# Expert down weights shared out among the DMA engines by neighbouring rows, in a two-layer streaming encoder

## The reference, cut to what matters

```python
def _swiglu(x, wa, wb, wc):
    return (jax.nn.silu(x @ wa) * (x @ wb)) @ wc
...
    for e in range(N_EXPERTS):
        y = y + comb[:, e:e + 1] * _swiglu(x, we1[e], we3[e], we2[e]).astype(f32)
```

## Time and profile before

| what | value |
|---|---|
| runs, us | 2668.35, 2989.45, 2655.33; median 2668.35 |
| the profiled execution, us | 2659.83 |
| its span, us | 2658.1 |
| TensorE busy | 2288.2 us (86%) |
| VectorE busy | 1534.9 us (58%) |
| ScalarE busy | 1157.2 us (44%) |
| memory read and written | 456.31 MB and 26.97 MB |
| chain that ended last, product lines L847 | 52% and 2% for L851 |

### The profile page before, as it was taken

The page is one execution under the profiler, slowest core; times in us unless marked ns, Lnnn a source line. Parts: engine busy times, 40 slices in busy tenths (PEclk is TensorE's granted clock), DMA queues, the critical chain, the costliest instruction groups (busy, mean ns, idle before and its releaser), DMA issues.

```text
span 2658.1 us, 37593 instructions
## 1 busy us (share of the span) xinstructions
PE 2288.2 (86%) x14153; PEld 1975.6 (74%) x14153; DVE 1534.9 (58%) x2150; ACT 1157.2 (44%) x1553; POOL 184.2 (7%) x257
## 2 busy tenths in 40 slices
PE   6899985778699989897999867587999999999991
PEld 3899753548599989897997635386878878878871
DVE  0456637323543444344566374336888888888884
ACT  3332113322443423333321134315777677777773
POOL 2000101101000000000000011100000100100104
PEclk7699766858799999996998678697999999999995
DMA  7122525351254444541223143305999999999993
GB/s 243 51 80 64 167 60 173 131 180 57 72 166 119 150 127 138 141 144 32 64 80 104 57 145 114 126 11 217 339 382 360 351 377 352 348 383 367 340 358 137
DMA packets 285625, 485.57 MB, mean 183 GB/s; under 512 B 21550, under 2 KB 216632, under 8 KB 285504
## 3 DMA queue, kind: packets, MB, share of 16 engines
q1 hardware_dynamic: 264816, 416.42, 45.3%
q0 software_dynamic: 20688, 67.44, 7.3%
HBM read 456.31 MB, written 26.97 MB: 182 GB/s over the span
## 4 chain that ended last, share of the span: by engine, by line
PE 54%; DVE 6%; DMA 6%; issue 3%; ACT 3%; POOL 1%; DVEq 0%; ACTq 0%; PEld 0%; PEldq 0%; POOLq 0%; SPq 0%
PE banks L847 52%; DMA expert_ring<-in_we 4%; PE banks L851 2%; ACT region_split L1572 1%; DVE region L2092 1%; DVE expert_lower L2092 1%; DVE weights_lower L2092 1%; DVE hidden_t L2092 1%; DVE scratch L2092 1%; ACT hidden_t L1572 0%; DVE region_split L2092 0%; DMA hidden_t<-h_rows,pass_tokens 0%; DMA scratch<-bias_rows 0%; DVE weight_ring L2092 0%; ACT scratch L1572 0%
## 5 line engine op out<-in xcount | busy, mean ns | idle before, releaser
L847 PE MATMUL banks<-upper_parts,region_split 128*128 128x320 f32 x1664 | 397.1, 314 | 37.0 <-DVE weights_lower L2092 29.3
L2092 DVE TENSOR_TENSOR expert_lower<-expert_ring,region_split 128x1408 fp32r<-128x1408 f32 (+1 forms) x270 | 388.6, 1467 | 28.1 <-ACT region_split L1572 18.5
L847 PE MATMUL banks<-upper_parts,weights_lower 128*128 128x320 f32 x1248 | 390.6, 313 | 0.0
L847 PE MATMUL banks<-region_split 128*128 128x320 f32 (+1 forms) x1376 | 376.6, 337 | 12.9 <-DVE upper_parts L2092 12.9
L1572 ACT ACTIVATE region_split<-expert_ring 128x1408 fp32r<-128x1408 f32 (+1 forms) x270 | 331.9, 1257 | 63.2 <-DMA expert_ring<-in_we 63.1
L847 PEld LDWEIGHTS banks<-upper_parts,region_split 128*128 128x128 f32 x1664 | 290.0, 192 | 38.8 <-DVE weights_lower L2092 35.8
L847 PE MATMUL banks<-region_split,upper_parts 128*128 128x512 f32 (+1 forms) x996 | 304.1, 382 | 1.4 <-DVE upper_parts L2092 1.4
L847 PE MATMUL banks<-z_weights_upper,upper_parts 128*128 128x256 f32 (+3 forms) x844 | 264.2, 342 | 22.6 <-DVE region_split L2092 22.5
L847 PE MATMUL banks<-expert_lower,upper_parts 128*128 128x512 f32 x720 | 271.4, 377 | 0.0
L847 PEld LDWEIGHTS banks<-region_split 128*128 128x128 f32 x1376 | 245.3, 189 | 28.8 <-issue 13.5
L1572 ACT ACTIVATE region_split<-weight_ring 128x2048 fp32r<-128x2048 f32 (+2 forms) x72 | 141.0, 1960 | 252.5 <-PE banks L847 225.2
(11 more groups left out here) (306 smaller groups left out, 3569.8 us busy)
## 6 DMA issues: line engine op xcount, KB each, us to landing
expert_ring<-in_we SPq DMA_DIRECT2D x240, 704.0 KB, 8.3
expert_ring<-in_we SPq DMA_DIRECT2D x165, 512.0 KB, 4.6
weight_ring<-in_w_ada SPq DMA_DIRECT2D x48, 1024.0 KB, 7.4
weight_ring<-in_w SPq DMA_DIRECT2D x88, 512.0 KB, 4.4
weight_ring<-in_w_in SPq DMA_DIRECT2D x24, 1024.0 KB, 5.3
weight_ring<-in_w SPq DMA_DIRECT2D x16, 1408.0 KB, 6.3
weight_ring<-in_w_out SPq DMA_DIRECT2D x8, 1024.0 KB, 8.8
y_rows<-hidden_t POOLq DMA_DIRECT2D x15, 512.0 KB, 7.5
```

What stands on the lines that cost most here:

```text
L847: return nc.tensor.matmul(out, lhsT, rhs, start=first, stop=last)
L2092: return v.tensor_tensor(out, x, y, op)
```

## The change

Two places. On SP, the down tiles' source is now a view with three dimensions: 16 groups (i), 8 rows in each (j), 1024 columns. Element (i, j) is row 128 f + 16 j + i of the expert's down weights, and it goes to partition 8 i + j. So a tile still has the same 128 rows of 4,096 B and goes to the same place of the ring, but its rows stand in another order: partitions 0 to 7 hold rows 0, 16, 32, ... 112 of the block, partitions 8 to 15 rows 1, 17, ... and so on.

On VectorE, the gated product's hidden columns are stored in that same order: position 8 i + j of block f holds hidden column 128 f + 16 j + i. Both inputs are read with a step of 16 elements for eight elements and then from the next column on; the output is contiguous. After the transpose partition 8 i + j of the turned product meets the row of the down tile that belongs to it.

The number of instructions and their order is the same on every engine. The 33 down loads in SP's program have one dimension more, and the three multiplications read with steps; nothing else differs.

```diff
--- before.py
+++ after.py
@@ -609,21 +609,23 @@
             l = DEPTH - 1
             sp.wait_ge(stage_done, 3 * (STAGES.index(f"out{l}") + 1))
             sp.wait_ge(slots_ready, 1)
-            by_row = [a[x][l // 2, :, :, :].rearrange("e (k p) n -> e p k n", p=P) for x in ("we1", "we3", "we2")]
+            by_row = [a[x][l // 2, :, :, :].rearrange("e (k p) n -> e p k n", p=P) for x in ("we1", "we3")]
+            down_rows = a["we2"][l // 2, :, :, :].rearrange("e (f j i) n -> e i j f n", j=8, i=16)
             n.add("expert_used", 1 - NPLACE)
             q = 0
 
             def expert_rows(e, up):
 
                 nonlocal q
-                w1, w3, w2 = (x[bass.ds(e, 1), :, :, :].rearrange("e p k n -> p (e k) n") for x in by_row)
-                for src in [w[:, k, :] for k in range(KD) for w in (w1, w3)] if up else [w2[:, f, :] for f in range(NF)]:
+                w1, w3 = (x[bass.ds(e, 1), :, :, :].rearrange("e p k n -> p (e k) n") for x in by_row)
+                w2 = down_rows[bass.ds(e, 1), :, :, :, :].rearrange("e i j f n -> i j (e f) n")
+                for src in [w[:, k, :] for k in range(KD) for w in (w1, w3)] if up else [w2[:, :, f, :] for f in range(NF)]:
                     if q >= NPLACE:
                         sp.wait_ge(expert_used, n.value("expert_used"))
                     n.add("expert_used")
                     place = q % NPLACE
                     q += 1
-                    sp.dma_start(ER[:, place, 0:src.shape[1]], src).then_inc(expert_in[place], 16)
+                    sp.dma_start(ER[:, place, 0:src.shape[-1]], src).then_inc(expert_in[place], 16)
 
             def expert_of(at):
                 return sp.value_load(PASSES[0:1, bass.ds(at, 1)], min_val=0, max_val=NE - 1)
@@ -2664,7 +2666,9 @@
                         for part, (first, end) in enumerate(PARTS):
                             take(silu_made)
                             take(ups_summed)
-                            tt(PRODUCT[:, first:end], SGM[:, first:end], PS[:, 3 + part, 0:end - first], ALU.mult)\
+                            turned = lambda x: x.rearrange("p (f j i) -> p f i j", j=8, i=16)
+                            tt(PRODUCT[:, first:end].rearrange("p (f i j) -> p f i j", j=8, i=16), turned(SGM[:, first:end]),
+                               turned(PS[:, 3 + part, 0:end - first]), ALU.mult)\
                                 .then_inc(product_made, 1)
 
                     def down(rows, products, following):
```

## The result

The changed kernel takes 2733.5 us at the median (2728.2 to 2741.2, four runs), the kernel before 2671.0 us beside it. The ratio, which leaves out one slow run of the kernel before (2989.5 us), is 1.0229, with an interval of [1.0185, 1.0272]: some 61 us slower. The forecast, 2638 us, has the wrong sign, and the time lies above its range, the high end of 2710 included. What happened has the signs of the rival of the landing side. The profiled execution took 2741.2 us, its span 2739.5 us.

What follows compares the result with a forecast made beforehand. TensorE was taken as the bound, stopped once a pass by late loads. From 2659.8 us, 21 for shorter stops and 3 for clock came off, 2 went back for strided reads: 2638 us, range 2618 to 2710 (forecast's own 2618 to 2655).

Steps and rivals of the forecast that it cites:

- What bounds the kernel before: Expert stage: TensorE bounds, 48.0 us of own work in a 50.64 us pass, stopping once a pass for late loads.
- the stops: TensorE's once-a-pass waits, 2.1 us each; shrinking them was to save 21 us, plus 3 us of low clock.
- (a): Down-tile loads: the new row order lifts them from 312 to 412 GB/s at full share, saving 21 us.
- landing-side rival: Down loads' writes: eight neighbouring partitions per engine make engines collide; under 300 GB/s decides, up to 2775 us; chance 0.33.
- In step half of the time: Landing-side rival's middle case: down tiles at 275 GB/s, 52.4 us of DMA a pass, 2685 to 2700 us.
- Engines drift apart: Argument against the landing-side rival: in a queue never empty, engines drift apart and then seldom meet.
- (b): Issue of down loads on SP: 40 ns more each, 0.4 us a pass, hidden by the queue's waits for TensorE.
- (c): VectorE's three strided gated products: +0.5 us a pass taken, +0.9 at most, hidden in 3.55 us of idle time.
- (d): Transposes, roundings and matrix products: same shapes and order, only the sum over rows reordered; no effect.
- VectorE becomes the bound: Rival: products grow 0.9 us a pass with nothing hiding them, 12 us in all, 2671 us; chance 0.05.
- Nothing: Rival: engines don't share loads as written, or down tiles' slowness comes from issue gaps; 2650 to 2668 us; chance 0.20.

Runs made afterwards that it cites:

- e1: The change's down loads with the gated product made as before (down part's result wrong), against the kernel before: ratio 1.0211.
- e10: All eleven down tiles in 16 groups of 8, ten with each group's rows adjacent in memory, product as before, against the kernel before: ratio 1.0237.
- e4: Down tiles' rows 11 apart from partition to partition, in the plain split of 128, TensorE turning every 11th product column, against the kernel before: ratio 0.9981.
- e7: Ten of eleven down tiles read 5,632 B from each row address, 4,096 B apart, against the kernel before: ratio 0.9953.
- e8: ScalarE and VectorE split the product's last part before the fourth up tile instead of behind it, against the kernel before: 2643.2 us, ratio 0.9891.
- e2: Down loads as before with the change's strided product (down part's result wrong), against the kernel before: ratio 0.998.

## Why the prediction was wrong, point by point

- **What bounds the kernel before: right.** The sum of 48.0 us a pass, the 2.6 us over it, and their cause (the splits of the product behind late up tiles) are confirmed by the earlier split: 48.4 us. The worth put on the stops, 21 + 3 us, was there to be had (28.7 us between the medians, ratio 0.9891), but not by this change.
- **(a) is the step that failed.** It took the upper of its two bounds, 412 GB/s; measured were 260 in one stretch, 244 over all passes by single packets, and 240 in stretches of e1 and e10 (246 and 247 at a share of 1.03): in the lower part between 206 and 412. The reason for the choice was that the down tiles' 312 GB/s at a full share come from where rows lie in memory. That is false: moved rows change next to nothing (e4, and e10 against e1), and 5,632 B from the same places run at 407 (e7). The 312 were 256 GB/s measured at a share of 0.82 and divided by 0.82. In that stretch the median row of 4,096 B takes 159 ns, which is 412 GB/s over 16 engines, as quick per byte as the up tiles' 215 ns for 5,632 B; a minority of long packets (one in ten over 301 ns) makes the mean 210. A stretch in which the queue keeps running dry doesn't hold the rate of a full one. At 48.4 us a pass and a share of 0.98 (e8) the DMA time is 47.5 us; less 28.0 and 3.4 that leaves 16.1 us for down tiles, 358 GB/s. That is an estimate (the rows' own mean in e8, 179 ns, gives 366); by it the down tiles' slowness per byte was half of what the prediction built on, and there was less to gain.
- **The landing-side rival: right in its signs, place and threshold, too cheap in the middle; its mechanism isn't shown.** Under 300 GB/s, landing after more than 6 us (8.3), ScalarE waiting in the down tiles, gathers over 52 us apart (54.2): each sign is in the profile. "In step half of the time" was priced at 275 GB/s, 52.4 us a pass, 2685 to 2700; measured, 260 GB/s and 54.2 us. The trace went beyond that price because the rate over all passes was lower still (244 GB/s by single packets), and by what a price for each pass doesn't contain: the stops at the end of the stage (+14.0 us from the last gather on). The Trainium skill's "SBUF — State Buffer", section "Door 1: The DMA port swizzle", has four neighbouring partitions on a port, and half of the rate for half of the ports. By that rule the passes would be 59.4 us; the trace has 54.2. A unit of four fits: 32 groups of 4 and 64 of 2 cost nothing (293 GB/s at 0.87, 309 at 0.90), 16 groups of 8 all of it. The half doesn't: 240 to 260 of 412 is 0.6. That the ports are what the engines share was not measured by itself.
- **The chances** gave 0.42 to a step whose reason was one division of a rate by its share, and 0.33 to the one that its own words called "for it: the DMA has almost no room". "Engines drift apart" was the weight against it, and no row carried that.
- **(b) right**: 333 ns, not the 40 ns more that it allowed.
- **(c)** The term was mis-sized: +0.5 us taken, +0.9 the upper bound, +1.0 measured. The upper bound came from a row without such steps, and its mean of 2,034 ns is one of two kinds: three of the five take 1.23 us and two take 3.25. The growth was hidden, as said (e2), and not in the ratio. The Trainium skill ("Vector Engine (DVE) Microarchitecture Reference", section 5.2) has 2.5 ns a column with both sources stepping 24 words. This case shows 2.05 ns with a step of 16 (1052/512). The estimate by that page, +2.1 us a pass, was twice what was measured, and my 0.5 us half of it.
- **(d) right**: TensorE's 60 products take 12.86 us before and after.
- "VectorE becomes the bound" (0.05): excluded by the product alone. "Nothing" (0.20): excluded by the result.

## What to carry to other kernels

The outermost count of a load's source can set its rate: here 32, 64 and 128 groups were equal within 0.5%, and 16 groups of 8 partitions lost a third or more of the rate, also for plain loads of the same size between them, so change a row order without changing that count. Don't turn a rate at a partial DMA share into the rate of a full queue; take it where the share is 1, or look at the median time of a single packet. And look first for short work that an engine could do before it waits for a load: moving two splits ahead of one tile gave 1.1% here, more than any order of the rows.

## What the runs showed of the hardware

- **A product in pairs reads nearly at full rate.** In 64 groups of 2 the product's inputs are read in the order 0, 64, 1, 65, ..., where no two that follow each other are adjacent. Mean of one (128 x 512), with 32 groups of 4 (steps of 32) beneath:

```profile
L2094 DVE TENSOR_TENSOR region<-region,banks 128x512 f32<-128x512 f32 x30 | 21.0, 710 | 11.4 <-PE banks L849 11.1 <-ACT region L1574 0.3
```

```profile
L2094 DVE TENSOR_TENSOR region<-region,banks 128x512 f32<-128x512 f32 x30 | 32.2, 1114 | 11.1 <-PE banks L849 10.8 <-ACT region L1574 0.3
```

  687 ns contiguous, 710 for pairs 64 apart, 1052 for eight 16 apart, 1114 for four 32 apart. The step alone doesn't set it; what does was not tried.
- A mixture of six slow and five plain tiles moved 328 GB/s, no more than all eleven slow (339); the plain ones between them took 246 to 261 ns a row, 170 to 209 before.
- All tiles in the slow split moved 287 GB/s at a full share, more than slow down tiles among plain up tiles (240 to 260).
